# Where the low parts of the weights begin in their ring slots, in a transformer block at float32 precision on one core

## The reference, cut to what matters

```
h    = rms_norm(x, ln_pre_mix)
proj = h @ w_in                       # 2048 x 7680: u, v, q, k, v, gate_a, gate_b
y_a  = gmlp_branch(gelu(u), gelu(v)) @ w_a_out
y_b  = swa_branch(q, k, v) @ w_b_out
mix  = (sigmoid(gate_a) * y_a + sigmoid(gate_b) * y_b) @ w_o
x    = x + rms_norm(mix, ln_post_mix)
up   = rms_norm(x, ln_pre_ffn) @ w_up        # 2048 x 16384
conv = causal depthwise conv, width 3, of up
x    = x + rms_norm((gelu(conv[:, :8192]) * conv[:, 8192:]) @ w_down, ln_post_ffn)
```

## Time and profile before

| | |
|---|---|
| median of three runs | 1588.19 us |
| profiled execution | 1588.61 us |
| its span | 1586.8 us |
| TensorE matmul busy | 1577.7 us (99% of the span) |
| TensorE weight load busy | 1367.8 us (86%) |
| VectorE busy | 1260.4 us (79%) |
| ScalarE busy | 828.1 us (52%) |
| mean HBM traffic | 197 GB/s |
| granted TensorE clock | 0.999 of full speed |

### The profile page before, as it was taken

How to read it: one execution, slowest core, us unless ns; L and a number is a source line. 1 busy time by engine, 2 the same in 40 slices (tenths; PEclk the granted TensorE clock), 3 DMA queues, 4 the chain that set the end, 5 groups by cost and what they waited for, 6 DMA issues and landing times.

```text
span 1586.8 us, 24342 instructions
## 1 busy us (share of the span) xinstructions
PE 1577.7 (99%) x8652; PEld 1367.8 (86%) x8652; DVE 1260.4 (79%) x1836; ACT 828.1 (52%) x1124; POOL 1.9 (0%) x12
## 2 busy tenths in 40 slices
PE   9999999999999999999999999999999999999998
PEld 8888888888888888888888888888888888888886
DVE  6556677677797788777787777877778899989999
ACT  6544544456565654444444444444444575766664
POOL 0000000000000000000000000000000000000000
PEclk9999999999999999999999999999999999999999
DMA  9895455556566465556555566655666555555552
GB/s 371 267 232 190 160 185 163 181 160 203 194 241 217 152 210 187 186 185 200 190 190 185 185 197 190 195 185 185 195 189 198 199 208 207 208 198 200 185 212 106
DMA packets 234946, 313.15 MB, mean 197 GB/s; under 512 B 5360, under 2 KB 209808, under 8 KB 234000
## 3 DMA queue, kind: packets, MB, share of 16 engines
q1 hardware_dynamic: 231056, 306.44, 58.5%
q10 hardware_dynamic: 3840, 6.05, 1.5%
HBM read 309.58 MB, written 2.88 MB: 197 GB/s over the span
## 4 chain that ended last, share of the span: by engine, by line
PE 96%; DVE 4%; issue 0%; ACT 0%; DVEq 0%
PE ps L1494 44%; PE ps L1498 23%; PE ps L1585 15%; PE ps L1778 6%; PE ps L1635 3%; PE ps L1598 1%; DVE actT L1189 1%; DVE w_lo L1189 1%; PE ps L1509 1%; PE ps L1514 0%; DVE arena L1177 0%; PE ps L1724 0%; PE ps L1705 0%; PE ps L1657 0%; PE ps L1717 0%
## 5 line engine op out<-in xcount | busy, mean ns | idle before, releaser
L1494 PE MATMUL ps<-actT,w_hi 128*128 128x512 f32 x3072 | 715.4, 390 | 0.0
L454 ACT ACTIVATE w_hi<-raw 128x1024 fp32r<-128x1024 f32 x420 | 433.4, 1056 | 509.0 <-PE ps L1494 256.9
L862 DVE TENSOR_TENSOR w_lo<-raw,w_hi 128x1024 fp32r<-128x1024 f32 x422 | 506.1, 1223 | 236.8 <-ACT w_hi L454 234.5
L1494 PEld LDWEIGHTS ps<-actT,w_hi 128*128 128x128 f32 x3072 | 569.4, 188 | 113.0 <-issue 0.2
L1498 PEld LDWEIGHTS ps<-actT,w_lo 128*128 128x128 f32 x3072 | 378.2, 188 | 9.9 <-issue 1.7
L1498 PE MATMUL ps<-actT,w_lo 128*128 128x256 f32 x3072 | 384.4, 281 | 0.0
L1585 PE MATMUL ps<-w_hi,xs 128*128 128x512 f32 x832 | 226.6, 389 | 0.0
L1585 PEld LDWEIGHTS ps<-w_hi,xs 128*128 128x128 f32 x832 | 156.1, 188 | 32.4
L1585 PE MATMUL ps<-w_lo,xs 128*128 128x512 f32 x416 | 128.1, 389 | 0.0
L1189 DVE TENSOR_TENSOR w_lo<-raw,w_hi 128x1024 fp32r<-128x1024 f32 x96 | 117.3, 1222 | 0.0
L1379 DVE SCALAR_TENSOR_TENSOR arena<-arena,convw 128x256 f32<-128x256 f32 x256 | 106.8, 480 | 0.0
(11 more groups left out here) (181 smaller groups left out, 935.7 us busy)
## 6 DMA issues: line engine op xcount, KB each, us to landing
raw<-in_w_up_dram SPq DMA_DIRECT2D x128, 1024.0 KB, 5.5
raw<-in_w_down_dram SPq DMA_DIRECT2D x64, 1024.0 KB, 5.2
raw<-in_w_in_dram SPq DMA_DIRECT2D x58, 1024.0 KB, 5.2
raw<-in_w_o_dram SPq DMA_DIRECT2D x16, 1024.0 KB, 5.3
raw<-in_w_a_out_dram SPq DMA_DIRECT2D x8, 1024.0 KB, 5.3
raw<-in_w_b_out_dram SPq DMA_DIRECT2D x8, 1024.0 KB, 5.2
arena<-in_x_dram SPq DMA_DIRECT2D x1, 2048.0 KB, 17.1
arena<-in_x_dram ACTq DMA_DIRECT2D x2, 1024.0 KB, 6.1
```

The source lines that it names most:

```text
L454: act.activation(w_hi[:, h % RING, :], raw[:, h // 2, h % 2 * HALF:(h % 2 + 1) * HALF], ACT.Copy)\
L862: dve.tensor_tensor(lo, raw[:, h // 2, h % 2 * HALF:(h % 2 + 1) * HALF], w_hi[:, h % RING, :].bitcast(F32), ALU.subtract).then_inc(lo_read ...
L1494: return pe.matmul(ps[:, bank + c, :], w_hi[:, h % RING, at:at + P], actT[:, k, :, :].rearrange("p a s -> p (a s)"), start=start, stop=stop)
```

## The change

The table of the four shifts holds other numbers. In slots 0, 1, 2 and 3 the low part begins 4, 12, 24 and 8 bytes behind the start of the slot, where it was 64, 32, 16 and 128 bytes. The writes of VectorE and the weight loads of TensorE follow, since both go through `w_lo_shifted`. The size of `w_lo` stays, and so do the addresses of all other tensors, the instructions of every engine and their order.

```diff
         w_lo_padded = sb("w_lo", [P, RING, HALF + P], F32R)
         w_lo = w_lo_padded[:, :, 0:HALF]
-        LO_SHIFT = (16, 8, 4, 32)
+        LO_SHIFT = (1, 3, 6, 2)
         w_lo_shifted = [w_lo_padded[:, slot, shift:shift + HALF] for slot, shift in enumerate(LO_SHIFT)]
```

## The result

| | before | changed |
|---|---|---|
| median (13 runs each) | 1588.42 us | 1591.99 us |
| lowest to highest | 1588.19 to 1588.72 | 1591.49 to 1592.43 |
| profiled execution, span | 1588.61, 1586.8 | 1591.84, 1590.0 |

The changed kernel is slower by 3.6 us: ratio 1.0022, 95% interval 1.0014 to 1.0030. The forecast was 1588.2 us with a range of 1583 to 1596, so the time lies in the range, but the mechanism that the forecast stood on (all starts other than zero cost the same) is wrong, as the experiments show.

The account below looks back on a forecast made before the run. The prediction took TensorE's matmul pace to bound the kernel. Its terms, 0 for VectorE's writes and 0 for the shifted loads, left the profiled 1588.61 us unchanged, 1588.2 us against the runs, range 1583 to 1596 us.

Parts of the forecast that it names:

- What bounds the kernel: Feature-major stages: TensorE's matmul pace sets the end; a nanosecond on each of 3072 narrow matmuls gives 3.07 us.
- The write of `w_lo`, 0: VectorE's 384 writes to the new addresses keep their duration and are hidden behind TensorE: 0 us.
- The load of the shifted block, 0: TensorE's 3072 loads of shifted low parts: no change of pace at the new non-zero starts, 0 us.
- some offset is better than none: Narrow matmuls: shifted ones 2 ns shorter than unshifted, while which offset hardly matters between 16 and 128 bytes.
- not touched: Wide matmuls of the feature-major stages: the change leaves them alone, 32 taking 7.27 us, 227.2 ns each.
- Times 96: Feature-major stages: 3072 / 32 = 96 periods of 11.05 us, 1061 us, by which a period's cost is multiplied.
- Small offsets count as none: Shifted loads: all 3072 fall back to unshifted durations, 2 ns each, 6.1 us more, 1594.3 us; chance 0.19.
- A load off the 16-byte grid reads one piece more: Shifted loads: 33 pieces for 32, 3.7 ns each, 11.3 us more, 1599.5 us; chance 0.09.
- the estimate that stood beside it: Shifted loads: an extra piece by the Trainium skill's 107 ns load costs 3.3 ns, 10.2 us in all.
- Finer offsets are better: Narrow matmuls: the new starts spare another 1.4 ns each, 4.3 us less, 1583.9 us; chance 0.19.
- Nothing of it is the offset: Narrow matmuls: short runs and waits explain the unshifted 2 ns; any offset worth 0; chance 0.53 together with the forecast.
- slots could differ: Narrow matmuls by slot: dearer slots 0 and 1 beside unchanged 2 and 3 would point to pieces of 8 bytes.

Follow-up runs that it names:

- the sweep: TensorE's matmuls alone on constant data, starts of the low parts varied, same in all slots: 32 narrow matmuls take 3.64 to 3.94 us.
- u1_slot2_back: Changed kernel with slot 2 alone put back from 24 to 16 bytes (starts 4, 12, 16, 8): 1588.35 us, 1.0001 of the kernel before.
- e1_zero: Kernel before with all four shifts set to 0, low parts at the start of their slots: 1594.88 us, ratio 1.0042.

## Why the prediction was right or wrong

- **What bounds the kernel.** Right. The changed stages run at PE's own pace: in the profiled executions PE's busy time and the span both grew by 3.2 us, and the sweeps with TensorE alone have the periods of the full kernel. That a nanosecond on each *narrow* matmul reaches the end whole does not hold: in u1_slot2_back the narrow run is 26 ns shorter and the wide one behind it 25 ns longer, and the time stays.
- **The write of `w_lo`, 0.** Right. The writes' durations are 1205/1224/1230 ns (min/median/max) after, against 1205/1224/1229 in the earlier trace rows; starts of 4, 8, 12 and 24 bytes show nothing. (384 of the 422 writes in these rows are shifted ones.)
- **The load of the shifted block, 0.** This is the step that failed. It said that "which offset it is hardly matters between 16 and 128 bytes", by the medians of eight durations. The start does matter, between 3.64 and 3.94 us for 32 narrow matmuls, a span of 9 ns each. Three of the four starts of before (64, 32 and 16 bytes) lie within 0.02 us of each other in the sweep, but the fourth, 128 bytes, takes 3.84 us and is no better than 0. So "some offset is better than none" was a wrong reading as well: in the sweep 128, 256 and 384 bytes are as slow as 0, and 24 and 204 bytes slower. The prediction read this off medians, and a median hides the two or three matmuls that are late, while the maximum (287 ns in slot 3) was there to see. That the time still came within 3.8 us of the forecast is luck in the choice of starts: slots 0 and 1 cost 0.5 us, slot 3 gave 0.5 back, and only slot 2 had a dear start, for 3.9. With all four at 24 bytes it would have been 10.0 us more, with all four at 76 it would have been 10.4 less.
- **The wide matmuls are "not touched".** Wrong as a term. Their operands are not, but 45 of the 53 ns a period are theirs. A wide run begins with two to nine slower matmuls in the full kernels, depending on the narrow run ahead of it; the sum by kind of instruction left this out.
- **Times 96.** The prediction multiplied by all 96 periods. The change costs 53 ns only where runs of 32 follow each other (72 periods, 3.8 us), and nearly nothing in the gates and in `y_turn`.
- **The rivals.** "Small offsets count as none" is refuted: 4 bytes give 3.78 us and 8 bytes 3.71, against 3.83 at 0. "A load off the 16-byte grid reads one piece more" is refuted by the sweep, where 256 bytes is slow and 76 fast; the estimate that stood beside it from figures of the Trainium skill (TensorE: Matmul & The Clock Gate, Weight-path perf modes and LDWEIGHTS) falls with it. "Finer offsets are better" is wrong as a trend, though 8 and 12 bytes are better than any of the old four. "Nothing of it is the offset" is refuted by e1_zero.
- **Size and chances.** The share given to no change (0.54) was high: with prices between -21.5 and +10.6 us and no row at any of the new starts, the forecast rested on one reading. Measured is slower, by a little more than the bound; the 0.26 for it stood on two rivals that are both refuted.
- **The sign "slots could differ".** The prediction asked to look slot by slot, and that is what found slot 2; its reading of it (dearer slots 0 and 1, pieces of 8 bytes) was wrong.

**What stays open.** Why 24 bytes is slow and 76 fast. Shown are the period of 256 bytes, that equal starts of weights and stream give the pace of 120 ns each (0, 24 and 76 bytes alike), and that the stream's start takes part. That the two reads get in each other's way in SBUF would fit this, but it is only argued; no run here separates it from another cause inside TensorE. The Trainium skill (TensorE: Matmul & The Clock Gate, Step-by-step) says that the two operands have independent read ports, so that a load takes nothing from the matmul under way. If the two never met, moving the stream would be worth the same whatever the start of the weights. The sweep does not agree: the stream's move from 0 to 76 bytes takes the run from 3.64 to 3.83 us under weights at 76, and from 3.83 to 3.74 under weights at 0. Also open is what a narrow run leaves behind that the next wide run needs up to nine matmuls to settle.

## What to carry to other kernels

Where TensorE is the bound and nothing waits, the address of a stationary float32 block within 256 bytes, against that of the stream, is a knob: here 20 us, 1.3%, lie between all four slots at 76 bytes and all four at 24. These runs show it for 128 by 128 blocks and streams of 256 and 512 columns. It follows no rule of size or alignment that these runs show, so measure it: a short program with only the matmuls, at the same shapes and in the same order, gave the full kernel's period to 0.01 us. Read spacings by slot and look at the maximum, not at the median of durations, and count the matmuls behind the changed ones too.

## What the runs showed of the hardware that was not expected

- With 256 streamed columns and 128 by 128 float32 blocks, the spacing of matmuls has no single floor: in steady runs it is 120 ns with equal starts and 113.3 ns at the best start (3.64 us for 32), by the position of the weights alone.
- The 512-column matmuls, at 227 ns in steady state, are slower by up to 7 ns each when their weights start elsewhere (7.51 against 7.28 us for 32), though there a load has about twice as long until the next one.
- Moving one slot's start by 8 bytes (16 to 24) cost 3.9 us of 1588, 0.24%, with the same instructions, data and waits.
